# RWKV chunk products of a streaming encoder step: from two diagonal 64x64 quarters and three groups to four quarters, chunk pairs and two groups

## What is computed

```python
def step(S, xs):                      # S: heads x 64 x 64, per frame
    rt, wt, kt, vt, kkt, at = xs
    sa = jnp.einsum('bhvk,bhk->bhv', S, -kkt)
    S = S * wt[:, :, None, :] + sa[..., None] * (kkt * at)[:, :, None, :] + vt[..., None] * kt[:, :, None, :]
    return S, jnp.einsum('bhvk,bhk->bhv', S, rt)
```

## Time and profile before

| | |
|---|---|
| median of 3 runs | 2813.71 us (2807.57 to 2817.39) |
| profiled execution, its span (no other time is given of it) | 2810.7 us |
| PE matmul busy, weight loads busy | 96%, 90% of the span |
| DVE, ACT, POOL busy | 60%, 27%, 9% |
| L1163, the products | 5184 + 1152 instructions, from 482 to 2103 us |
| mean granted clock of TensorE | 0.992 |

### The profile page before, as it was taken

How to read it: one execution, slowest core, us unless ns; L and a number is a source line. 1 busy time by engine, 2 the same in 40 slices (tenths; PEclk the granted TensorE clock), 3 DMA queues, 4 the chain that set the end, 5 groups by cost and what they waited for, 6 DMA issues and landing times.

```text
span 2810.7 us, 63639 instructions
## 1 busy us (share of the span) xinstructions
PE 2702.0 (96%) x26656; PEld 2539.2 (90%) x26656; DVE 1687.1 (60%) x3103; ACT 755.9 (27%) x1813; POOL 245.4 (9%) x423
## 2 busy tenths in 40 slices
PE   8999999999999999999989999999999998999998
PEld 7877889999999889999988788899999997999997
DVE  6645565666666576664485456466666656666634
ACT  2243343333332320000123434332233324100001
POOL 1221111000000100000002211110000000000000
PEclk9999999999999999999999999999999999999999
DMA  5454436222263223233235444442224532223231
GB/s 162 130 141 123 128 106 165 74 73 66 77 179 113 61 78 91 84 89 90 83 100 150 112 128 149 74 157 73 74 70 117 157 98 76 76 85 89 87 90 60
DMA packets 421293, 290.29 MB, mean 103 GB/s; under 512 B 38560, under 2 KB 387392, under 8 KB 420880
## 3 DMA queue, kind: packets, MB, share of 16 engines
q1 hardware_dynamic: 399024, 228.64, 29.3%
q0 software_dynamic: 21984, 57.59, 6.5%
HBM read 232.12 MB, written 54.07 MB: 102 GB/s over the span
## 4 chain that ended last, share of the span: by engine, by line
PE 78%; DVE 10%; DVEq 3%; ACT 3%; DMA 3%; issue 2%; ACTq 0%; SPq 0%
PE PS L762 35%; PE PS L858 11%; PE PS L1163 8%; PE PS L1096 7%; DMA U<-gate_scratch 2%; ACT U L1425 1%; PE PS L904 1%; PE PS L1137 1%; PE PS L1305 1%; PE PS L783 1%; ACT U L1428 1%; PE PS L940 1%; DVE WLO L2458 1%; DVE WLO L1946 1%; PE PS L1021 1%
## 5 line engine op out<-in xcount | busy, mean ns | idle before, releaser
L762 PE MATMUL PS<-U_r,WHI 128*128 128x272 f32 x3008 | 535.5, 289 | 14.1 <-DVEq L2459 9.0
L1936 DVE CAST WHI<-ring 128x1024 fp32r<-128x1024 f32 (+2 forms) x262 | 175.2, 669 | 490.9 <-PE PS L762 362.6
L762 PEld LDWEIGHTS PS<-U_r,WHI 128*128 128x128 f32 x3008 | 435.8, 188 | 20.3 <-DVEq L2459 13.3
L1428 ACT COPY U<-PS 128x272 f32<-128x272 f32 (+8 forms) x770 | 266.5, 373 | 658.4 <-PE PS L1163 139.9
L762 PE MATMUL PS<-brT_r,WHI 128*128 128x272 f32 x1920 | 397.7, 288 | 7.4 <-DVEq L1948 6.0
L762 PE MATMUL PS<-U_r,WLO 128*128 128x272 f32 x1728 | 355.6, 287 | 0.0
L762 PE MATMUL PS<-hT_r,WHI 128*128 128x272 f32 x1600 | 330.2, 288 | 0.0
L1946 DVE TENSOR_TENSOR WLO<-ring,WHI 128x1024 fp32r<-128x1024 f32 (+2 forms) x262 | 308.2, 1176 | 21.4 <-issue 1.8
L762 PE MATMUL PS<-brT_r,WLO 128*128 128x272 f32 x1536 | 317.8, 288 | 0.0
L762 PEld LDWEIGHTS PS<-brT_r,WHI 128*128 128x128 f32 x1920 | 301.2, 188 | 10.0 <-DVEq L1948 7.5
L762 PEld LDWEIGHTS PS<-U_r,WLO 128*128 128x128 f32 x1728 | 270.0, 188 | 0.0
(11 more groups left out here) (351 smaller groups left out, 4105.4 us busy)
## 6 DMA issues: line engine op xcount, KB each, us to landing
ring<-in_w_in_dram SPq DMA_DIRECT2D x126, 512.0 KB, 4.4
ring<-in_w_ffn_in_dram SPq DMA_DIRECT2D x88, 512.0 KB, 3.8
ring<-in_w_ffn_out_dram SPq DMA_DIRECT2D x32, 448.0 KB, 3.5
proj_scratch<-U POOLq DMA_DIRECT2D x104, 136.0 KB, 2.1
U<-proj_scratch SPq DMA_DIRECT2D x48, 272.0 KB, 4.3
ring<-in_w_branch_dram SPq DMA_DIRECT2D x48, 256.0 KB, 3.2
gate_scratch<-U POOLq DMA_DIRECT2D x88, 136.0 KB, 3.3
U<-gate_scratch SPq DMA_DIRECT2D x44, 272.0 KB, 2.9
```

The costliest lines, as they stand in the source:

```text
L762: ins = mm(PS[:, 2 * q + h, 0:HT], w, half(x, h), start=(first and k == 0 and n == 0), stop=(last and k == kn - 1 and n == len(terms) - 1))
L1428: return act.copy(out, in_)
L1936: copy(hi, src)
```

## The change

Chunks are taken in pairs (2j, 2j+1). Group 0 has the pairs 0 and 1 (chunks 0 to 3), group 1 the pairs 2 to 4 (chunks 4 to 8, the fifth pair has one chunk only). A product is issued per pair as four matmuls, over two halves of rows and two halves of columns. `to_chunks` reads operands with a head in each half of the partitions and writes results with a chunk in each half, `to_heads` the reverse, `in_chunks` stays within a chunk's half. So operands alternate between the two layouts; those that came from products with an identity (`st`) are now made by 20 transposes at the start (`turned`), which ACT and DVE copy. The groups have four banks each, "side 0" read by DVE and "side 1" by ACT.

```diff
+        def banks(gr, side, at, step, n):
+            nj = RW_PAIRS[gr][1] - RW_PAIRS[gr][0]
+            b, o = 4 * gr + 2 * side, at % step
+            return PS[:, b:b + 2, at - o:at - o + step * nj].rearrange("p x (j n) -> p x j n", j=nj)[:, :, :, o:o + n]
...
-                        def three(gr, bank, at, step, pairs):
...
+                        def products(gr, bank, at, step, order, rows, cols, *terms, first=True, kept=False):
+                            for j in range(*RW_PAIRS[gr]):
+                                o = at + step * (j - RW_PAIRS[gr][0])
+                                for n, (w, x) in enumerate(terms):
+                                    for a in order if j < 4 else tuple(a for a in order if a[0] == 0):
+                                        r, c = halves[a[rows]], halves[a[cols]]
+                                        x_a = x(j, a)[r]
+                                        ins = mm(PS[c, bank(a), o:o + x_a.shape[-1]], w(j, a)[r], x_a,
...
+                        QUADS, HEADS = ((0, 0), (1, 1), (0, 1), (1, 0)), ((0, 0), (1, 1), (1, 0), (0, 1))
+                        def to_chunks(gr, side, at, step, *terms):
+                            return products(gr, lambda a: 4 * gr + 2 * side + a[1], at, step, HEADS, 1, 0, *terms)
+                        def to_heads(gr, side, at, step, *terms, first=True, kept=False):
+                            return products(gr, lambda a: 4 * gr + 2 * side + a[0], at, step, QUADS, 0, 1, *terms,
+                                            first=first, kept=kept)
+                        def in_chunks(gr, side, at, step, *terms):
+                            return products(gr, lambda a: 4 * gr + 2 * side + a[1], at, step, QUADS, 0, 0, *terms)
...
                             if s == 1:
-                                three(gr, b0, 0, 128, [(B, AR)])
-                                ins = three(gr, b1, 0, 128, [(K, AR)])
+                                to_chunks(gr, 0, 0, 128, (B, A))
+                                ins = to_chunks(gr, 0, 64, 128, (K, A))
                             if s == 2:
-                                three(gr, b0, 0, 64, [(A, B)])
-                                three(gr, b0, 192, 64, [(V, st)])
-                                three(gr, b1, 0, 64, [(A, st)])
-                                ins = three(gr, b1, 192, 64, [(B, st)])
+                                to_chunks(gr, 0, 0, 64, (A, B))
+                                ins = in_chunks(gr, 1, 0, 64, (KA, Vt))
...
                             if s == 10:
-                                ins = three(gr, b0, 0, 128, [(W, GB)])
+                                to_heads(gr, 0, 0, 64, (W3, Bt), kept=True)
+                                to_heads(gr, 1, 0, 64, (W3, GTt), kept=True)
+                                to_heads(gr, 0, 192, 64, (Bt, Y3), (Kt, Vt), first=False, kept=True)
+                                ins = to_heads(gr, 1, 192, 64, (Y3, GTt), (Vt, HTt), first=False, kept=True)
...
+                        for i, bank in enumerate((4, 5, 6, 7)):
+                            if bank >= 6:
+                                pe.wait_ge(gt_evac, l * 48 + 2 * (q0 + 2) + bank - 6 + 3 + it * 16)
+                            for j in range(4):
+                                ins = turned(sources[i](2 * j, 2), bank, j * P, 2)
+                            ins.then_inc(rw_turned, 1)
                         for s in range(1, 11):
-                            for gr in range(3):
+                            for gr in range(2):
+                                if gr == 1 and s < 3:
+                                    pe.wait_ge(rw_tput, g * 4 + 2 * s)
                                 stage(s, gr)
...
                             if c >= 1:
-                                pe.wait_ge(rw_chain, g * 10 + c)
...
+                                pe.wait_ge(rw_chain, g * 10 + (c + 1 if c < 8 else 1))
+                                chained(c, 0, MR[:, c, 0:64], ST[:, c, :]).then_inc(rw_state, 1)
+                                ins = chained(c, 1, ST[:, c, :], MR[:, c, 64:128])
...
                             if s == 7:
-                                copy(MM[gr], bank(0, 0, 2))
+                                copy(to_head(WY1, gr, 0, 128), banks(gr, 1, 0, 128, 128))
+                                act.wait_ge(rw_ev[gr], g * 12 + 8)
+                                copy(to_head(MT, gr, 0, 64), banks(gr, 0, 64, 128, 64))
```

More of the change, by code:

```diff
@@ L118 @@
 GROUP = 32
+RW_PAIRS = ((0, 2), (2, 5))
 DIFF_TILES = (4, 0, 1, 2, 3)
@@ L131, in constants @@
     put("ident", np.eye(P))
-    put("stack", np.tile(np.vstack([i64, i64]), (1, 3)))
+    put("stack", np.tile(np.hstack([i64, -1.0 * i64]), (2, 1)))
     put("bdones", np.kron(np.eye(2), np.ones((64, 64))))
@@ L144, in constants @@
     same = r // 16 == s // 16
-    for name, m in (("up_d", -1.0 * ((r < s) & same)), ("up_s", r < s), ("up_i", r <= s),
-                    ("lo_d", -1.0 * ((r > s) & same)), ("lo_o", (r > s) & ~same)):
-        put(name, np.tile(np.vstack([m, m]), (1, 3)))
+    put("up", np.tile(np.hstack([-1.0 * ((r < s) & same), r < s]), (2, 1)))
+    for name, m in (("up_i", r <= s), ("lo_d", -1.0 * ((r > s) & same)), ("lo_o", (r > s) & ~same)):
+        put(name, np.vstack([m, m]))
     put("reset", (np.arange(TP) % CHUNK != 0)[None, :])
@@ L1167, in stage @@
-                        def stage(s, gr):
[L1168 to L1183, removed]
@@ L1224, in _, with chained @@
                                 stage(s, gr)
+                        def chained(c, side, w, x):
+                            bank, o = chunk_at(c)
+                            for r in halves:
+                                ins = mm(PS[r, bank + 2 * side, o:o + 64], w[r], x[r], start=False, stop=side == 1,
+                                         skip_group_check=True)
+                            return ins
                         for c in range(9):
-                            gr, cc = divmod(c, 3)
@@ L1711, in evac @@
+                        for i, to in enumerate(turned_to):
+                            act.wait_ge(rw_turned, g * 5 + i + 2)
+                            copy(to[:, 0:4], PS[:, 4 + i, :].rearrange("p (j h n) -> p j h n", j=4, h=2))
+                            act.drain().then_inc(rw_tput, 1)
+                        gate_cast(q0 + 4, it)
                         def evac(s, gr):
-                            def bank(i, at, k=1):
-                                return PS[:, 2 * gr + i, at:at + 192 * k].rearrange("p (i c n) -> p i c n", i=k, c=3)
@@ L1729, in evac @@
+                            if s == 9:
+                                copy(to_chunk(WY3, gr, 0, 128), banks(gr, 1, 0, 128, 128))
                             act.drain().then_inc(rw_eva[gr], 1)
@@ L2393, in evac @@
                             if s == 7:
-                                copy(wy, bank(1, 0, 128))
+                                m = banks(gr, 0, 0, 128, 64)
+                                copy(to_head(MH, gr, 0, 64), m)
+                                tt(to_head(IM, gr, 0, 64), spread(plus, m), m, ALU.subtract)
                             if s == 8:
-                                tt(wy, wy, bank(1, 0, 128), ALU.subtract)
+                                tt(to_chunk(M2I, gr, 0, 64), spread(minus, a), a, ALU.subtract)
@@ L2403, in evac @@
+                                for q in range(2):
+                                    c = slice(4 * gr + q, (4, 9)[gr], 2)
+                                    n = (2, 3 - q)[gr]
+                                    r_ = PS[:, 4 * gr + 2 + q, 0:64 * n].rearrange("p (j n) -> p j n", n=CHUNK)
+                                    tt(MR[:, c, 64:128], r_, KR[:, 1, c, :], ALU.add)
                             dve.drain().then_inc(rw_ev[gr], 1)
+                        plus, minus = const("stack")[:, 0:64], const("stack")[:, 64:128]
```

252 lines of the change are left out of this document (131 added, 121 removed).

## The result

The changed kernel takes **2850.89 us** (median of 4 runs, 2847.97 to 2855.28), the kernel before 2815.53 us on the same chip: a ratio of 1.0136, 95% interval 1.0119 to 1.0154. It is slower by 35 to 38 us, where 25 us less were forecast. The gap to explain is some 61 us, 7.6 us in each of the eight blocks.

The account below looks back on a forecast made before the run. PE bounds the kernel, its products by rounds of instructions. Per block: products -9.5, transposes +2.2, waits +3.6, chain -0.4, so -4.1; eight blocks -33, clock +8, sum -25 us: 2789 us, range 2768 to 2820.

Parts of the forecast that it names:

- So a round costs what one tile costs ... I take 58.5 ns: RWKV products: four matmul instructions on four quarters take as long as one tile, 58.5 ns for 64 columns, 110 for 128.
- 270 narrow and 40 wide rounds: Products of a block, in sets of four instructions of 64 or 128 columns: 20.2 us instead of 29.7, -9.5 us.
- rival B: Products: TensorE cannot be fed if starts are limited to 29.2 ns; decides from about 22 ns; 2874 us, chance 0.20.
- so I cost the cast at nothing: ScalarE's moved 1.05 us weight cast behind the transposes' copies: hidden, 0 us; without cover up to 1 us a block.
- Waits, +3.6 us a block: Products: with two groups, PE waits between stages for wider DVE and ACT copies, +3.6 us a block, bounds 1.5 to 6.
- The chain, −0.4: State chain: fewer calls per step leave links of 0.72 us, 7.05 us against 7.53, -0.4 us a block.
- The clock: TensorE falls to half speed around each chain's end because links are thin: about 1 us a block, +8 us.

Follow-up runs that it names:

- Experiments 5 and 6: Changed kernel with, in 5, narrow products merged (288 instructions fewer a block, same columns): 1.0069, 2831.77 us; in 6, 144 calls a block widened to 128 columns: 1.0136, 2851.71 us.
- Experiment 1: Changed kernel with ScalarE's count for stage 1 given ahead of the weight cast instead of behind it: 1.0113, 2842.74 us.
- experiment 4: Changed kernel with small unread products in the state chain: two calls per link, 1.0088, 2836.35 us; a second kernel with twelve at the second link, 1.0096, 2838.31 us.

## Why the prediction was wrong

- **"So a round costs what one tile costs ... I take 58.5 ns"** held between stops: in the first block, stages of narrow products on all four quarters and without a stop ran at 15.0 to 17.0 ns a matmul (32 in 0.48 us, 48 in 0.71), and all stages together took 158.8 us where rounds alone give 161.6. The step that failed is the next, unwritten one: that a stage is made of rounds alone. 270 narrow and 40 wide rounds need 1044 loads and 1044 matmuls in 20 us, about 8 packets of 256, one in 2.5 us; none of the trace's packets follows another by less than 3.3 us. Before the change the same count is 1584 instructions in 29.7 us, one packet in 4.8 us. **Missing term: the supply of instructions, which the sum has at nothing: 36 stops, 44.3 us from start to start (36.3 us idle).** Experiments 5 and 6 separate it from columns: it falls with the instructions at equal columns (−19 us), and columns are partly free at equal instructions.
- This is **rival B**, "TensorE cannot be fed", in another form. The products took 29.3 ns a matmul with all stops and waits, where B had 29.2 for the issue alone; that the two agree is chance. Without the waits it is 24.3 ns, past the 22 that the prediction names as the sign of B, but single starts are not limited to it. B was given 0.20 and 2874 us. The argument against it fell short: that the columns explain a round's interval of 58.5 ns says nothing of a supply that is needed for 20 us on end.
- The Trainium skill (TensorE: Matmul & The Clock Gate, "Wait — 56ns, not 53.3ns?") gave about 2839 us, an estimate by a floor of about 25 ns between starts, and it is the number nearest to 2851. As a rule on starts it does not hold here: the first four matmuls of the products start within 20 ns. The prediction says that no row shows it or rules it out, but the trace of the kernel before did: the four column tiles of L697 start at 0, 7, 14 and 20 ns, and the two quarters of L1163 7 ns apart. As a mean over packets it nearly holds: 256 instructions in 3.3 us are 26 ns a pair. That 2839 comes near is therefore partly luck; it has neither the cast nor the clock's full price in it.
- **"so I cost the cast at nothing"** failed by 13.4 us from start to start, 11.7 us idle. The first copy ScalarE owes is indeed that of stage 2, but not the first count: PE's stage 2 waits for `rw_eva` of stage 1, which the empty `skip` gives behind the cast. The text named the price if the cover were gone, up to 1 us a block; it was 1.5 idle, since the four copies ahead end at 487.26, later than PE's stage 1 too. Experiment 1 shows it: without the cast ahead 2.3 us are left.
- **Waits, +3.6 us a block:** right. The copies took what was estimated to within some nanoseconds, and the intervals between stages come to 27.8 us, 3.5 a block. Single ones differ: before stage 8 of group 1 it was 1.36 us in most blocks against 1.0, before stage 2 of group 1 nothing against 0.2.
- **The chain, −0.4:** shown only with the clock held, 6.70 us against the 6.7 worked out. At the lower clock it cost 7.21.
- **The clock:** that it falls around each chain came true, and in six blocks as forecast, in the thin chain; in the other two a stop of the products stood just before, which the forecast did not have. 8 us were set and 15 measured (experiment 4), just above the upper end of 14. The sum had 0.3 to 0.4 us a block for the links and up to 0.9 for the sums and rounded to 1; the runs show 0.5 in the chain, 0.2 from the final state to the sums, and 1.1 of the last 1.2 in the sums. The gates behind them cost next to nothing, as forecast.
- Together: in the products 44 us of stops and 13 of the cast stand against 3 us less in the stages and 1 less between them, 54 us with rounding; the clock cost 7 us more than was set. To a microsecond or two that is the gap of 61.

## What to carry to other kernels

Before a product is spread over more tiles, count its instructions as well as its columns, and compare the pace that they then need with the densest pace that any long stretch of the trace has sustained; a few starts that follow closely are no proof of supply. Here 72 calls fewer in a block, with the same columns, were worth 19 us of 2850. When an instruction is moved on an in-order engine, look for what it is moved in front of, and count the instructions that only signal. When a latency chain is made thin, price the clock for all that stands behind it, and keep small products at hand for filling. And compare like with like: idle time in a profile starts at the modelled end of a matmul, a forecast in intervals at its start.

## What the runs showed of the hardware that was not expected

- Instructions reach TensorE in packets of 16384 bytes. Their starts are 3.3 us and more apart in a dense stretch, 34 of 34 stops end 2.2 to 3.0 us after one, and the stops of a block lie 126 or 127 matmuls apart, or two or three times that. One can see it as idle time "<-issue" in the middle of a run of matmuls. That the packets' latency is the cause, and not something that goes with them, was not tested by itself; the number of instructions was.
- Four 64x64 quarters run at 15 ns a matmul of 64 columns in bursts, and take their instructions out of the program's order between quarters: with the calls in another order starts stayed 16 to 21 ns apart, more than two quarters were at work, and the time did not change (1.0143 against 1.0136).
- 288 matmuls a block were made twice as wide at no measurable cost (1.0136 both), though PE was busy for 27.5 us more: the stops and waits shrank by 27.9 us.
- After stretches with PE busy for 1.27 to 1.95 us of 3.4 the granted clock fell, in all eight blocks; it cost 1.9 us a block; two calls more at each link kept it in five of eight, and twelve at the longest wait in all.
